# Gating one tile ahead and two output tiles inside the last RWKV tile, in a hybrid attention and RWKV-7 encoder layer

## The chip, the cores and the metric

The kernel runs on one core of a Trainium2 chip. The metric is the device time of one execution in microseconds (us). The engines are PE (TensorE, with PEld its weight loads), DVE (VectorE), ACT (ScalarE), POOL (GpSimd) and SP (SyncE, which here only issues DMAs). Each runs its own instructions in the order in which they were written, and they meet at semaphores.

## What is computed

One layer of a hybrid streaming encoder, for a prompt of 2048 rows and for eight running streams of 16 rows (128 sample rows). The input is normalised and projected once; half of the columns feed a chunked attention of 8 heads, the other half an RWKV-7 recurrence of 8 heads, and both results are gated and projected back.

```python
proj = rms_norm(h_p, norm_gain[l]) @ w_in[l]
att, rcols, g_r = split_projection(proj)
q, k, v, g_a = attn_qkv(att, q_norm_gain[l], k_norm_gain[l])
o_a = chunk_band_attention(q, k, v, rel_pos_bias[l])
o_r, S_p = rwkv_branch(rcols, prev, zeros, g_r, *rw)
h_p = h_p + merge_out(o_a, g_a, o_r, w_out[l], h_p.dtype)

def wkv_scan(...):          # the recurrence, one step per row and head
    sa = jnp.einsum('bhij,bhj->bhi', S, -kk_t)
    S = (S * w_t[:, :, None, :] + sa[..., None] * (kk_t * a_t)[:, :, None, :]
         + v_t[..., None] * k_t[:, :, None, :])
    y = jnp.einsum('bhij,bhj->bhi', S, r_t)

def merge_out(o_a, g_a, o_r, w_out, dtype):
    z = jnp.concatenate([o_a * jax.nn.silu(g_a), o_r], axis=-1)   # o_r holds its own silu gate
    return z @ w_out
```

The sample rows go the same way, each stream from its own cached keys, values and state.

## The kernel before, in words

All is float32. Large products are made as three: each operand is split into a high part (rounded by a copy on ACT) and a low part (what is left, by a subtraction on DVE or POOL), and hi·hi, hi·lo and lo·hi are added in PSUM. A block of 8 slices of 128 by 512 columns is so 24 products.

There are four phases in order, and between them each engine meets the others at a barrier while POOL clears the semaphores that the phase held (`clear_semaphores`, L64 to L74; the clear itself at L66 in the rows). If the numbers held are consecutive, one instruction clears the range; otherwise one instruction clears each.

1. `attention_phase` (to about 588 us): projection, attention over the prompt.
2. `rwkv_projection_phase` (589 to 901): the RWKV columns. On ACT its head loads the sigmoid table (L971), then splits weights and input.
3. `rwkv_phase` (904 to 1634, clears to 1640.4), described below.
4. `output_phase` (from 1640.5): for each of 17 tiles of 128 rows, the gated z is turned (PE L2311), split (ACT L2198, DVE L2236), multiplied by `w_out` (PE L2318, 48 products), added to the input (DVE L2245) and stored. ACT makes the silu (L2193), DVE the gating (L2232). Eight of the tiles also carry the attention of one sample stream each (L2330 to L2349).

`rwkv_phase` has 17 tiles: 16 of 128 prompt rows and the sample tile (`DEC` = 16, mode "s"). For each engine small generators write the instructions of parts of a tile: `mix` (decay, key gate, the sum for kk), `front` (scaled keys, Gram matrices), `back` (the recurrence itself), `tail` (group norm, bonus, y), `gates` (the silu gates' projection, 48 products in 12 blocks of 4, PE L2036). A generator yields a number, the place in the tile in us, ahead of each piece; `merged` (L1075) always takes the piece with the smallest number next. These numbers alone set the order of instructions on each engine; `tiles` (L1313) says which parts of which tiles run together: `back(t)`, `tail(t-1)`, `front(t+1)`, `mix(t+2)` and `gates(t+2)` (`AHEAD` = 2). Ahead of the first tile `first_gates` makes the gates of tiles 0 and 1, and the last four of the eight splits of the gate weights (ACT L1634, DVE L1802).

`back(t)` begins with the levels: five of them (three in the sample tile), each a product w (PE L1927), its mask (DVE L1737), a product q (PE L1936), a copy y_mat (ACT L1589) and a transpose of it (DVE L1741), so that one level goes round three engines. Then for both chunks of 64 rows come the right hand side, the solve (PE L1963), the state product (PE L2000), the state add on DVE and the read-out (PE L1970). In the sample tile each stream has its own state: DVE masks rows by stream (L1766), PE multiplies by all states (L1952), and at the end PE L2019 and DVE L1776, L1780 renew them.

Level 0 of the next tile needs at its front: z (DVE L1726, a masking with two SBUF inputs, behind POOL's `bm` L1477), y2 (DVE L1729, a transpose of z), and on PE, in order ahead of it, the turns of v (L1838, L1841), which need kk_n (DVE L1675) read first. The gate of the tile is copied by ACT (L1618), then the next x is rounded on ACT (L1613) and its low part made on POOL (L1521; on DVE L1808 in the prologue); the first gate block of the next tile waits for that part.

`tail(t)` is DVE L1786 to L1794, ACT L1602 to L1607, POOL L1501 to L1516, then four stores on SP. Tiles 15 and 16 have no gates; in their place `out` splits `w_out` (ACT L1647, DVE L1814), four slices in each, and in tile 16 it makes silu (ACT L1652) and the gating (DVE L1821) for output tiles 0 and 1, whose inputs SP loads (L1404 to L1406). `z_att` holds the o_att and o_rwkv rows.

## Time and profile before

| what | value |
|---|---|
| median of 3 runs (lowest, highest) | 1881.86 us (1880.72, 1885.09) |
| profiled execution, own time | 1879.3 us |
| its span | 1877.5 us |
| mean granted clock of PE | 0.968 |
| busy: PE, PEld, DVE, ACT, POOL | 93%, 76%, 46%, 42%, 18% |

The page divides the span into 40 equal slices of 46.9 us; each digit is a share in tenths (9 is 90% or more), PEclk the granted clock of PE:

```
PE   6999999999999997999999699999999999976389999
DVE  4345454445544412223445655566555665223432
ACT  4455655555555412223434444444434432014321
POOL 3010100100100000000214443345334532200000
PEclk9999999999999999999899999999999999986689999
```

Times of instructions are taken from one profiled execution and counted from the start of its span. A share of busy time is a mean over stages that have different limits, so each stage is read for itself. In a timeline, `[0.84 <-POOL gate_x_lo L1521]` says that the engine had been idle for 0.84 us and which event ended that.

### The profile page before, as it was taken

Reading aid. Unit: us, or ns where it says so; the run is one execution under the profiler, and the core shown is the slowest. Engines: PE = TensorE matmul, PEld = TensorE weight load, DVE = VectorE, ACT = ScalarE, POOL = GpSimd, SP = SyncE. Lnnn points to the kernel's source line nnn. Section 1 sums busy time; section 2 is a strip of 40 time slices with the busy share of each in tenths; the row PEclk is TensorE's granted clock in tenths of the full one; section 3 lists DMA queues with packets and bytes.
Section 4 is the critical chain, followed back from the end, with each engine's and each line's share of the span. In section 5 each row is a group of like instructions: output and inputs, shape, how many; then the busy total and the mean of one; then the engine's idle time right before and its main releaser. Section 6 shows DMA issues by size and latency. Waiting matters only on the chain. (4 is left out here: it accounts for less than half of the span.)

```text
span 1877.5 us, 48788 instructions
## 1 busy us (share of the span) xinstructions
PE 1740.1 (93%) x21474; PEld 1428.1 (76%) x21474; DVE 854.9 (46%) x1211; ACT 784.2 (42%) x1678; POOL 342.3 (18%) x249
## 2 busy tenths in 40 slices
PE   6999999999997999999699999999999976389999
PEld 4677778877886888999577777777777766267787
DVE  4345454445544412223445655566555665223432
ACT  4455655555555412223434444444434432014321
POOL 3010100100100000000214443345334532200000
PEclk9999999999999999999899999999999986689999
DMA  6010101101115322224212221121112123166642
GB/s 225 28 52 34 51 29 35 51 29 56 52 35 191 131 101 87 81 81 131 107 49 67 66 60 49 53 81 56 54 50 84 39 59 110 37 218 210 235 162 101
DMA packets 110977, 160.84 MB, mean 86 GB/s; under 512 B 36272, under 2 KB 73520, under 8 KB 110512
## 3 DMA queue, kind: packets, MB, share of 16 engines
q1 hardware_dynamic: 101408, 143.25, 23.3%
q10 hardware_dynamic: 9360, 14.49, 2.1%
q8 instruction: 170, 2.79, 0.6%
q14 instruction: 39, 0.32, 0.1%
HBM read 103.18 MB, written 55.05 MB: 84 GB/s over the span
## 5 line engine op out<-in xcount | busy, mean ns | idle before, releaser
L625 PE MATMUL a_ps_proj<-a_w_hi,a_x_hi 128*128 128x512 f32 x384 | 158.5, 413 | 2.9 <-ACT a_qk L374 2.8
L625 PE MATMUL a_ps_proj<-a_w_hi,a_x_lo 128*128 128x512 f32 x384 | 158.8, 414 | 0.0
L625 PE MATMUL a_ps_proj<-a_w_lo,a_x_hi 128*128 128x512 f32 x384 | 156.5, 408 | 0.0
L1045 DVE SCALAR_TENSOR_TENSOR j_out<-j_ps,j_rest,j_part 128x512 f32<-128x512 f32 (+2 forms) x65 | 41.9, 644 | 217.0 <-ACT j_last_cols L991 169.9
L2036 PE MATMUL r_ps_gate<-gate_w_hi,gate_x_hi 128*128 128x512 f32 x272 | 116.1, 427 | 21.4 <-POOL gate_x_lo L1521 11.8
L304 POOL TENSOR_TENSOR a_x_lo<-a_xT,a_x_hi 128x1024 fp32r<-128x1024 f32 x17 | 41.5, 2442 | 483.8 <-ACT a_x_hi L360 456.8
L2036 PE MATMUL r_ps_gate<-gate_w_hi,gate_x_lo 128*128 128x512 f32 x272 | 119.6, 440 | 0.0
L2036 PE MATMUL r_ps_gate<-gate_w_lo,gate_x_hi 128*128 128x512 f32 x272 | 115.8, 426 | 0.0
L2318 PE MATMUL o_ps_y<-out_w_hi,o_z_hi 128*128 128x512 f32 x272 | 111.5, 410 | 4.0 <-DVE o_y L2245 4.0
L524 DVE SCALAR_TENSOR_TENSOR a_stage<-a_ps_s,a_old_bias 128x1024 f32<-128x1024 f32 (+3 forms) x60 | 66.9, 1115 | 93.1 <-PE a_ps_s L652 93.1
L2318 PE MATMUL o_ps_y<-out_w_hi,o_z_lo 128*128 128x512 f32 x272 | 107.6, 395 | 0.0
L2318 PE MATMUL o_ps_y<-out_w_lo,o_z_hi 128*128 128x512 f32 x272 | 107.6, 395 | 0.0
L989 ACT ACTIVATE j_part<-j_last_cols,j_shift_in 128x1 f32<-128x1 f32 x65 | 19.2, 295 | 210.3 <-PE j_ps L1070 210.3
L1737 DVE TENSOR_TENSOR r_w_mat<-r_ps_w,consts 128x512 f32<-128x512 f32 x83 | 57.3, 691 | 106.8 <-PE r_ps_w L1927 106.8
L411 ACT ACTIVATE a_stage<-a_stage,a_small 128x640 f32<-128x640 f32 (+4 forms) x128 | 95.8, 752 | 2.1 <-DVE a_small L530 2.1
L421 ACT ACTIVATE a_stage<-a_ps_p 128x512 f32<-128x512 f32 (+3 forms) x120 | 60.1, 553 | 71.1 <-PE a_ps_p L671 71.0
L625 PEld LDWEIGHTS a_ps_proj<-a_w_hi,a_x_hi 128*128 128x128 f32 x384 | 72.9, 190 | 21.1 <-ACT a_qk L374 5.4
L652 PE MATMUL a_ps_s<-a_kT,a_qT 64*128 64x128 f32 (+3 forms) x592 | 83.0, 391 | 3.9 <-ACT a_kT L402 1.4
L1070 PE MATMUL j_ps<-j_x_hi,j_w_lo_ 128*128 128x384 f32 (+1 forms) x240 | 85.5, 356 | 0.0
L1070 PE MATMUL j_ps<-j_x_hi,j_w_hi_ 128*128 128x384 f32 (+1 forms) x240 | 85.5, 356 | 0.0
L1070 PE MATMUL j_ps<-j_x_lo,j_w_hi_ 128*128 128x384 f32 (+1 forms) x240 | 85.5, 356 | 0.0
L530 DVE TENSOR_REDUCE a_small<-a_stage 128x2 f32<-128x1280 f32 (+4 forms) x64 | 84.5, 1320 | 2.2
(302 smaller groups left out, 4406.5 us busy)
## 6 DMA issues: line engine op xcount, KB each, us to landing
xs<-scratch_xs_T SPq DMA_DIRECT2D x17, 832.0 KB, 6.2
scratch_xT<-a_xT SPq DMA_DIRECT2D x17, 512.0 KB, 4.7
raw<-scratch_xT SPq DMA_DIRECT2D x17, 512.0 KB, 7.6
scratch_gates<-r_gate_out SPq DMA_DIRECT2D x34, 256.0 KB, 2.4
z_gate<-scratch_gates SPq DMA_DIRECT2D x17, 512.0 KB, 4.5
a_x<-in_x_prompt SPq DMA_DIRECT2D x16, 512.0 KB, 4.5
o_x<-in_x_prompt SPq DMA_DIRECT2D x16, 512.0 KB, 4.8
out_y_prompt<-o_y SPq DMA_DIRECT2D x16, 512.0 KB, 2.9
```

The source lines that it names most:

```text
L304: nc.gpsimd.tensor_tensor(x_lo[n % 2][:], xT[:], x_hi[n % 2][:].bitcast(F32), ALU.subtract).then_inc(x_lo_ready, 1)
L411: nc.scalar.activation(probs[s % 2][:, e, lo * P:WIN], probs[s % 2][:, e, lo * P:WIN], ACT.Exp, bias=neg_max[s % 2][:, e:e + 1], accum_out ...
L421: nc.scalar.activation(pT[:, e, lo:SLOTS - 1, :], ps_p[:, e * 512 + lo * P:(e + 1) * 512].rearrange("p (j n) -> p j n", n=P), ACT.Copy).th ...
L524: nc.vector.scalar_tensor_tensor(out=out[:, :, lo * P:OLD], in0=ps_old[:, :, lo * P:OLD], scalar=SCALE, in1=old_bias[:, 2 * c:2 * c + 2, l ...
L530: nc.vector.tensor_reduce(neg_max[s % 2], out[:, :, lo * P:WIN], AX_X, ALU.max, negate=True).then_inc(max_ready, 1)
L625: mm = nc.tensor.matmul(ps_proj[:], a[n % 2][:, k, :], w[:, k, g * AW:(g + 1) * AW], start=(k == 0 and i == 0), stop=(k == KT - 1 and i == 2))
L652: return nc.tensor.matmul(out, qT[half, c, :], kT[half, c, r:r + b - a, :].rearrange("p j n -> p (j n)"), start=True, stop=True)
L1045: last = nc.vector.scalar_tensor_tensor(out=out[j][:, 0:n], in0=ps[j][:, 0:n], scalar=rest[:, c:c + 1], in1=part[j][:, 0:n], op0=ALU.mult, ...
L1070: mm = nc.tensor.matmul(ps[j][:, 0:n * P], w[c][:, k, :], x[g % 2][:, k, 0:n, :].rearrange("p a n -> p (a n)"), start=(k == 0 and m == 0), ...
L1737: nc.vector.tensor_tensor(w_mat, heads(ps_w[:]), level, ALU.mult).then_inc(w_ready, 1)
L2036: mm = nc.tensor.matmul(ps_gate[:], x[:, k, :], w[:, j, k, :], start=i == 0, stop=i == 3 * KT - 1)
L2318: mm = nc.tensor.matmul(ps_y[t % 2][:, cols], a[t % 3][:, k, :], w[:, k, cols], start=(k == 0 and i == 0), stop=(k == KT - 1 and i == 2))
```

## The change

- `clear_semaphores` clears each run of consecutive numbers with one instruction, however the numbers lie.
- Projection phase: the load of the sigmoid table moves from ahead of the first weight split to behind the second.
- `AHEAD` is 1. The prologue makes tile 0's gate only, and two of its four weight splits move ahead into the first stage of the prologue (22.5, 24), two to the second (10.2, 14.5). In each tile t from 0 to 15 the gates of t+1 are made. The last two gate blocks move from 30 and 31.5 to 28.9 and 30. kk_n (DVE) moves from 33.4 to 32.45, so that it stands ahead of y2.
- Tile 15 makes the gates of tile 16 where it split `w_out`. All eight splits of `w_out` stand in tile 16, with four buffers for the loads.
- In tile 16, `out` makes output tiles 0 and 1 whole: loads of gates and of both o, silu, gating, 16 transposes in groups of 4, splits, 96 products in blocks of 4 at the places of `OUT_AT` (two halves of 512 columns each, in the banks of the gate and of a job), the addition of x, and four stores. In the same tile z of output tiles 2 and 3 is prepared as that of 0 and 1 was. The second chunk's stream masks get the place 23, the two products for the new states 40 and 44.
- `output_phase` begins at tile 2, with the first sample stream on its second tile instead of its third.

```diff
             numbers = sorted(sem.num for sem in held)
-            if numbers[-1] - numbers[0] == len(numbers) - 1:
-                pool.sem_clear(range(numbers[0], numbers[-1] + 1))
-            else:
-                for sem in held:
-                    pool.sem_clear(sem)
+            first = numbers[0]
+            for now, after in zip(numbers, numbers[1:] + [None]):
+                if after != now + 1:
+                    pool.sem_clear(range(first, now + 1))
+                    first = after
...
-        self.out_w_loaded, self.out_w_hi, self.out_w_lo = [sem(f"out_w_loaded{i}") for i in range(2)], sem("out_w_hi"), sem("out_w_lo")
+        self.out_w_loaded, self.out_w_hi, self.out_w_lo = [sem(f"out_w_loaded{i}") for i in range(4)], sem("out_w_hi"), sem("out_w_lo")
...
-            act.preload_act_table_set("sigmoid_and_others")
             split_w(0)
             for k in range(KT):
                 split_x(0, k)
             split_w(1)
+            act.preload_act_table_set("sigmoid_and_others")
...
-        FIRST_GATES = ([(0, 0, 10)] + [(0, b, 16 + b) for b in (1, 2, 3)] + [(0, 4, 33)],
-                       [(0, 5, 10), (0, 6, 10.5), (0, 7, 12), (0, 8, 13)] + [(0, b, 10 + b) for b in (9, 10, 11)] +
-                       [(1, 0, 23), (1, 1, 23.5), (1, 2, 24)] + [(1, b, 23 + b) for b in (3, 4, 5)] + [(1, 6, 30), (1, 7, 30.5), (1, 8, 31)] +
-                       [(1, 9, 32), (1, 10, 33), (1, 11, 34)])
-        FIRST_GATES_OUT = ([], [(0, 0, 11), (0, 1, 22), (1, 0, 28.9), (1, 1, 34.5)])
-        GATE_W_AT = (13, 19, 22, 24)
-        OUT_AT = {DEC - 1: (5, 10, 15, 33), DEC: (1.5, 5.6, 9.7, 13.8)}
-
-        def out_blocks(t):
-            return range(4) if t == DEC - 1 else range(4, KT)
+        FIRST_GATES = ([(0, 10), (1, 17), (2, 18), (3, 19), (4, 33)],
+                       [(5, 10), (6, 10.5), (7, 12), (8, 13), (9, 19), (10, 20), (11, 21)])
+        GATE_W_AT = ((22.5, 24), (10.2, 14.5))
+        OUT_AT = (12, 13, 14, 15, 16, 17, 26.3, 26.4, 26.5, 33, 34, 35, 36, 37, 41, 42, 43, 43.5) + tuple(45 + i for i in range(6))
...
-        AHEAD = 2
+        AHEAD = 1
...
-                    run.append(out(t, u, "p"))
+                    run.append(out(t, u, "s"))
...
-            load_gate_x(2)
...
+            def load_out_w(k):
+                sp.dma_start(out_raw[k % 4][:].rearrange("p k n -> p (k n)"), io["w_out"][0, k * P:(k + 1) * P, :]).then_inc(shared.out_w_loaded[k % 4], 16)
+
+            def load_go(n, gate_loaded, att_loaded):
+                rows, b = slice(n * P, (n + 1) * P), n % 2
+                sp.dma_start(z_gate[b][:].rearrange("p g n -> p (g n)"), io["gates"][rows, :]).then_inc(gate_loaded, 16)
+                sp.dma_start(z_att[b][:, 0, :], io["o_att"][rows, :]).then_inc(att_loaded, 16)
+                sp.dma_start(z_att[b][:, 1, :], io["o_rwkv"][rows, :]).then_inc(att_loaded, 16)
...
+            def first_out():
+                for name in ("B1", "K1", "bonus", "kk_sum"):
+                    was_written(sp, DEC + 1, name)
+                for j in range(2):
+                    sp.wait_ge(gate_stored[j], 16 * 4)
+                sp.wait_ge(o_stored, 64 * 4)
+                load_go(0, go_loaded[0], go_loaded[0])
+                load_out_w(2)
+                load_out_w(3)
+                load_go(1, go_loaded[1], go_loaded[1])
...
+                yield 0
+                for k in range(4, KT):
+                    sp.wait_ge(shared.out_w_lo, k - 3)
+                    load_out_w(k)
+                for j in range(2):
+                    sp.wait_ge(gate_stored[j], 16 * (DEC + 1))
+                    load_x_half(0, j)
+                yield 19
+                for n in range(2):
+                    sp.wait_ge(z_turned, 2 * n + 2)
+                    load_go(2 + n, shared.g_loaded[n], shared.o_loaded[n])
+                for j in range(2):
+                    yield 31 + j
+                    store_y(0, j)
+                    sp.wait_ge(y_stored[j], 16)
+                    load_x_half(1, j)
...
+            def open_gates(n, loaded, opened):
+                act.wait_ge(loaded, 48 if loaded is go_loaded[n % 2] else 16)
+                nc.scalar.activation(z_gate[n % 2][:], z_gate[n % 2][:], ACT.Silu).then_inc(opened, 1)
...
+                yield 0.2
+                split_w(0)
+                split_w(1)
+                yield 1.4
+                open_gates(0, go_loaded[0], z_opened)
+                open_gates(1, go_loaded[1], z_opened)
+                yield 3.4
+                split_w(2)
+                split_w(3)
+                for n in range(2):
+                    for i in range(2):
+                        yield 6 + 2 * n + i
+                        round_z(n, i)
+                for k in range(4, KT):
+                    yield 10 + k
+                    split_w(k)
+                for n in range(2):
+                    yield 33 + n
+                    open_gates(2 + n, shared.g_loaded[n], shared.silu_ready)
...
-                yield 33.4
+                yield 32.45
...
+                            yield 23
...
+                yield 0.3
+                split_w(0)
+                split_w(1)
+                for n in range(2):
+                    yield 3 + n
+                    gate(n, z_gate[n], z_opened, z_gated)
+                yield 5.2
+                split_w(2)
+                split_w(3)
+                for n in range(2):
+                    for i in range(2):
+                        yield 6.4 + 2 * n + i
+                        split_z(n, i)
+                for k in range(4, KT):
+                    yield 10.5 + k
+                    split_w(k)
+                yield 27
+                add_x(0, 0)
+                yield 36
+                add_x(0, 1)
+                for n in range(2):
+                    yield 34 + n
+                    dve.wait_ge(shared.o_loaded[n], 32)
+                    gate(2 + n, z[n], shared.silu_ready, shared.z_ready)
...
+            for j in range(2):
+                add_x(1, j)
...
+                        yield (40, 44)[n]
...
-                for j, keys in enumerate(((1.1, 3.2, 5.2, 7.3, 9.3, 11.4), (13.4, 17.5, 19.6, 23.6, 30, 31.5))):
+                for j, keys in enumerate(((1.1, 3.2, 5.2, 7.3, 9.3, 11.4), (13.4, 17.5, 19.6, 23.6, 28.9, 30))):
...
+                def products(n, j, b):
+                    for i in range(4 * b, 4 * b + 4):
+                        k, m = divmod(i, 3)
+                        if i == 0:
+                            wait(pe, y_added, 2 * (n - 1) + j + 1)
+                            if n == 0:
+                                pe.wait_ge(z_lo_ready, 4)
+                                pe.wait_ge(gate_copied, 2 * (DEC + 1))
+                        if n == 0 and j == 0 and m == 0:
+                            pe.wait_ge(shared.out_w_lo, k + 1)
+                        a, w = ((z_hi, out_hi), (z_hi, out_lo), (z_lo, out_hi))[m]
+                        mm = nc.tensor.matmul(out_bank(j)[:], a[n][:, k, :], w[:, k, OUT_X[j]], start=i == 0, stop=i == 3 * KT - 1)
+                    if b == 5:
+                        mm.then_inc(y_summed, 1)
+
+                for n in range(2):
+                    for i in range(2):
+                        yield 6 + 2 * n + i
+                        turn(n, i)
+                for b, key in enumerate(OUT_AT):
+                    yield key
+                    products(b // 12, b // 6 % 2, b % 6)
...
-        FIRST = 2
+        TILE0, STREAM0 = 2, 1
+        LAST = DEC - TILE0
...
-            z_high(1)
-            silu(2)
-            z_high(2)
-            silu(3)
-
-            for t in range(FIRST, DEC + 1):
-                if t + 1 <= DEC:
+            for t in range(LAST + 1):
+                if t + 1 <= LAST:
...
-            turn(1)
             pe.wait_ge(w_lo_ready, KT)
-            for t in range(2):
-                pe.wait_ge(z_lo_ready, t + 1)
-                for j in range(2):
-                    for k in range(KT):
-                        products(t, j, k)
-            turn(2)
-
-            for t in range(FIRST, DEC + 1):
+            for t in range(LAST + 1):
```

In `out` on PE, `turn` waits for z_gated and the bank (`B1`, `K1` read, later z_lo of the group before), transposes four slices and signals z_turned. On ACT and DVE `round_z` and `split_z` make the high and low parts of each group of four slices, and `add_x(n, j)` adds the bank to the half of x that SP loaded. The PE part of `output_phase` no longer has its first two tiles ahead of the loop.

## Rows read from the trace of the kernel before

**Rows 1.** Windows: stretch, length, busy (x count) per engine, clock, DMA share, GB/s

```profile
1220.49:1258.42 37.93, 36.60 (x877) 29.40 (x868) 22.45 (x36) 17.08 (x36) 16.30 (x13) 1.00 0.21 60
1525.33:1563.07 37.74, 25.70 (x745) 23.95 (x737) 25.42 (x36) 13.11 (x24) 9.92 (x7) 0.76 0.24 72
1563.07:1602.29 39.22, 25.96 (x580) 24.40 (x582) 23.06 (x25) 9.88 (x15) 11.19 (x7) 0.62 0.33 105
1640.50:1675.96 35.46, 28.28 (x120) 23.42 (x121) 6.49 (x8) 6.35 (x6) 1.84 (x4) 0.84 0.48 174
904.00:953.86 49.86, 39.94 (x420) 29.80 (x424) 23.13 (x29) 21.97 (x42) 15.70 (x15) 0.87 0.25 91
```

**Rows 2.** Chain that ended last: start, length, engine, tile, line, count

```profile
1644.31 1.24 DVE o_z_lo L2236
...
1647.61 23.50 PE o_ps_y L2318 x96
...
1796.36 10.93 PE o_ps_y L2318 x48
```

**Rows 3.** SP queue's waits (total, times, longest), 1560 to 1700, then 580 to 600

```profile
SPq L66 <- PEq L66: 6.7, 1, 6.7
...
SPq L66 <- PEq L66: 0.5, 1, 0.5
```

**Rows 4.** Timeline, ACT, projection head: start, length, line, tiles, count, [idle, releaser]

```profile
589.00 1.28 ACT L971 ACT_TABLE_LOAD   x1 [4.63 <-PEq L66]
```

**Rows 5.** Timeline, DVE and POOL, prologue of the RWKV phase (904 to 955)

```profile
916.37 3.72 DVE L1802 TENSOR_TENSOR gate_w_lo<-raw,gate_w_hi 128x1024 fp32r<-128x1024 f32 x2 [0.70 <-ACT gate_w_hi L1634]
...
948.27 1.28 POOL L1463 TENSOR_TENSOR r_kmod<-xs,r_fac 128x512 f32<-128x512 f32 x1
...
948.35 1.75 DVE L1726 TENSOR_TENSOR r_z_mat<-r_bm,consts 128x512 f32<-128x512 f32 x1 [0.68 <-POOL r_bm L1477]
```

**Rows 6.** Waits of PE, 950 to 1525: waiter, releaser, total, times, longest

```profile
PE r_ps_gate L2036 <- POOL gate_x_lo L1521: 11.8, 14, 0.8
```

**Rows 7.** Timeline around one tile boundary (1215 to 1223): PE, DVE, POOL

```profile
1215.44 0.40 PE L2036 MATMUL r_ps_gate<-gate_w_lo,gate_x_hi 128*128 128x512 f32 x1
1215.77 0.68 PE L2000 MATMUL r_ps_s<-r_u_tok,r_b_tok 64*64 64x64 f32 x16
...
1218.05 0.39 PE L2036 MATMUL r_ps_gate<-gate_w_hi,gate_x_lo 128*128 128x512 f32 x1
...
1222.50 0.50 PE L2036 MATMUL r_ps_gate<-gate_w_hi,gate_x_hi 128*128 128x512 f32 x1 [0.84 <-POOL gate_x_lo L1521]
...
1217.29 0.69 DVE L1726 TENSOR_TENSOR r_late<-r_late,consts 128x512 f32<-128x512 f32 x1
...
1218.65 0.65 DVE L1675 TENSOR_SCALAR r_kk_n<-r_ps_job 128x512 f32<-128x512 f32 x1
...
1220.09 2.35 POOL L1521 TENSOR_TENSOR gate_x_lo<-raw,gate_x_hi 128x1024 fp32r<-128x1024 f32 x1 [3.89 <-ACT gate_x_hi L1613]
```

**Rows 8.** Timeline of tile 16 (1563 to 1634): ACT, DVE, POOL

```profile
1567.87 0.60 ACT L1589 ACTIVATE r_y_mat<-r_ps_q 128x512 f32<-128x512 f32 x1 [6.21 <-PE r_ps_q L1936]
...
1591.72 1.28 ACT L1652 ACT_TABLE_LOAD   x1
1593.01 2.00 ACT L1652 ACTIVATE z_gate<-z_gate 128x1024 f32<-128x1024 f32 x2
...
1579.37 5.03 DVE L1766 TENSOR_TENSOR r_late<-r_ar,consts 128x512 f32<-128x512 f32 x4
...
1594.99 1.21 DVE L1814 TENSOR_TENSOR out_w_lo<-raw,out_w_hi 128x1024 fp32r<-128x1024 f32 x1
...
1616.18 0.69 DVE L1776 TENSOR_TENSOR r_states<-r_states,r_ps_s 128x512 f32<-128x512 f32 x1 [7.23 <-PE r_ps_q L2019]
...
1627.93 1.26 POOL L1516 TENSOR_TENSOR r_y_tok<-r_y_tok,r_y_sq 128x512 f32<-128x512 f32 x1
```

**Rows 9.** DMA issues of 1565 to 1620: count, KB each, median us to landing

```profile
z_att<-scratch_o_rwkv SPq DMA_DIRECT2D x2, 256.0 KB, 7.0
```

More of the change, by code:

```diff
@@ L1437, in _ @@
             tiles(sp, nothing, back, mix, tail, gates, first_gates, out)
+            for j in range(2):
+                store_y(1, j)
+            for j in range(2):
+                sp.wait_ge(y_stored[j], 16 * 2)
             sp.wait_ge(stored, 16 * (1 + NCH))
@@ L1810, in out, with add_x, split_w @@
+                if t == 1:
+                    yield 24.6
+                    dve.wait_ge(x_hi_ready, 2)
+                    nc.vector.tensor_tensor(x_lo[:], x_raw[1][:], x_hi[:].bitcast(F32), ALU.subtract).then_inc(x_lo_ready, 1)
+            def add_x(n, j):
+                dve.wait_ge(y_summed, 2 * n + j + 1)
+                dve.wait_ge(x_half_loaded[j], 16 * (n + 1))
+                nc.vector.tensor_tensor(gate_out[j][:], gate_out[j][:], out_bank(j)[:], ALU.add).then_inc(y_added, 1)
             def out(t, u, mode):
-                for k in out_blocks(t):
-                    yield OUT_AT[t][k % 4] + 1.1
+                def split_w(k):
@@ L2047, in first_gates, with out, turn @@
             def first_gates(t, u, mode):
-                for n, b, key in FIRST_GATES[t]:
+                for b, key in FIRST_GATES[t]:
                     yield key
-                    gate_products(n, b // 6, b % 6)
-            tiles(pe, front, back, mix, gates=gates, first_gates=first_gates)
+                    gate_products(0, b // 6, b % 6)
+            def out(t, u, mode):
+                def turn(n, i):
+                    pe.wait_ge(z_gated, n + 1)
+                    if n == 0:
+                        was_read(pe, DEC, ("B1", "K1")[i])
+                    else:
+                        pe.wait_ge(z_lo_ready, 2 * n - 1 + i)
+                    for k in range(4):
+                        last = nc.tensor.transpose(ps_job[i][:, k * P:(k + 1) * P],
+                                                   z_gate[n][:].rearrange("p g d -> p (g d)")[:, (4 * i + k) * P:(4 * i + k + 1) * P], ident)
+                    last.then_inc(z_turned, 1)
+                def products(n, j, b):
[3 more added lines that the diff above has]
+                            wait(pe, y_added, 2 * (n - 1) + j + 1)
+                            if n == 0:
+                                pe.wait_ge(z_lo_ready, 4)
[13 more added lines that the diff above has]
+                    products(b // 12, b // 6 % 2, b % 6)
+            tiles(pe, front, back, mix, gates=gates, first_gates=first_gates, out=out)
 def output_phase(nc, io, shared):
@@ L2280, in _ @@
             split_z(0)
-            split_z(1)
-            apply(2)
-            split_z(2)
-            place_queries()
-            add(0, 0)
-            add(0, 1)
-            add(1, 0)
-            for t in range(FIRST, DEC + 1):
-                add(t - 1, 1)
-                if t + 1 <= DEC:
+            for t in range(LAST + 1):
+                if t > 0:
+                    add(t - 1, 1)
+                if 2 <= t + 1 <= LAST:
                     apply(t + 1)
@@ L2299, in _ @@
                     bias_and_max(b)
-                if t + 1 <= DEC:
+                if t + 1 <= LAST:
                     split_z(t + 1)
+                if t == 0:
+                    place_queries()
                 add(t, 0)
-            add(DEC, 1)
+            add(LAST, 1)
         @block.tensor
```

160 lines of the change are left out of this document (78 added, 82 removed).

## The prediction

> **What bounds the kernel now.** The profiled execution took 1879.3 us for a span of 1877.5 us; the median of the runs is 1881.86 us, 2.6 above it. All sums are differences on that execution, and I apply the total to the median.
>
> I read the 40 slices first (they stand in the section on the profile: PE at nine tenths nearly everywhere, with a hole from 1500 to 1690), then the stretches of the RWKV phase in a table by windows [rows 1], then the timeline around each hole, engine by engine. A steady RWKV tile lasts 37.93 us and PE is busy for 36.60 of them: it is bound by PE. The last two tiles are not. Tile 15 has PE busy for 25.70 of 37.74 at a granted clock of 0.76, tile 16 (the sample tile) for 25.96 of 39.22 at 0.62; here the level chain, going round PE, DVE and ACT, sets the time. Then come the last states, the tail and the store, 6.7 us with nothing on any engine, and 35.46 us until the output phase starts its third tile. The output phase itself is a chain on PE alone: 48 products in 10.93 us, 0.227 each [rows 2].
>
> **Output phase.** It loses tiles 0 and 1 from its head: 96 products in 23.50 us, their turns, and the wait for add, turn and split of tile 2. Before, tile 2's first product starts 35.46 us after the phase does [rows 1]. Now tile 2 is what tile 0 was: its low part is written 1644.31 + 1.24 = 5.1 us after the phase's start at 1640.5 [rows 2]. Gain 35.46 - 5.1 = 30.4. The clock's climb costs about the same in both (96 products took 23.50 where 96 x 0.227 = 21.8). Eight stream tiles and seven plain ones follow in either kernel. The loads lie closer to their first use; landing within 8 us of issue (the slowest like row is 7.0 [rows 9]) they keep ahead of tile 3, 15 us in. Bounds 27 to 32.
>
> **Semaphore clears.** Before the output phase, the queue of SP waited 6.7 us; at the same point after the attention phase, whose numbers are consecutive, 0.5 [rows 3]. By runs, the RWKV phase should cost like the latter: gain 6.2. If the numbers lie scattered, nothing; I know no reason for more than a few runs.
>
> **Projection's head.** ACT loads its table for 1.28 us before the first weight split, with PE idle behind it [rows 4]. Moved behind the second split, it delays only the third split, which PE wants ten us later. Gain 1.3.
>
> **Prologue.** Two things. The four weight splits no longer stand ahead of the first tile's chain on DVE (two of them took 3.72 us [rows 5]): the scan starts 3 us earlier, but the first two now sit in front of kk_n and the other two lengthen ACT's and DVE's queues in the next stage, so 2.6 us remain at the turns of b. Then the whole of tile 1's gate (48 products, 10.9 us by [rows 2]) is gone from between the turns and level 0, 13.5 together. The work behind it shows through: ACT's copies of k, of the gate and of b and the split of x, five times 512 columns at 0.6 [rows 8], and on DVE the masking of z, 1.75 behind POOL as now [rows 5], and kk_n. Laid end to end these are 5.4; walked through the Gram steps and the turns, 5.0 of them lie bare. Level 0 starts at 945.3 where it now starts at 953.86 [rows 1]. Gain 8.5; bounds 7 and 11.
>
> **Steady tiles.** Now PE waits at each tile's head for POOL's low part of x: 11.8 us in 14 tiles [rows 6]. The last two gate blocks move ahead of the solve and ahead of the state product, so the gate is copied and x split sooner and this wait goes. But the state product comes later, and with it the state add, z, kk_n and the turns that must precede level 0. Let L be the start of the last gate product. The state product follows at L + 0.33 (as 1215.44 to 1215.77), z at 1.52 behind it (1215.77 to 1217.29), L + 1.85; kk_n, now ahead of y2, at z's end, 0.64 later; level 0, behind the turns, 1.84 after kk_n (1218.65 to 1220.49): L + 4.33 [rows 1, 7]. Counting the blocks that move ahead of it, I put L at 1216.7 where the row has 1218.05, so level 0 starts at 1221.05 (now 1220.49), and the next gate block at 1222.2 (now 1222.50). Gain 0.3 per tile, 14 times, and 0.7 at the boundary before tile 15, which now has z lengthened by POOL: 4.9. Bounds 0 and 10.
>
> **Tile 15** gains a gate (11 us of PE) in 12 us of idle PE, a full clock, and loses four w_out splits that made PE wait. The levels become those of a steady tile. Less the mix of a tile 17 that does not exist and plus DVE's slower sample forms I estimate 36.7 against 37.74: gain 1, bounds -1 and 3.
>
> **Tile 16** takes it all up: 96 products (21.8 us), 16 transposes, all eight w_out splits, four z rounds, four splits, four gate products, two silu pairs, four adds and all their DMAs. T is the start of its level 0, before at 1563.07 [rows 1]. The places where it ends up on the path:
> - ACT waits in order for the gates of both tiles. SP can issue them only behind the last gate's store; with w_out's blocks between, tile 1's last load is issued at T + 1.2 and lands after 7.0 [rows 9]: T + 8.2. The silu follows, and only then the first y_mat copy, at T + 9.3 instead of 4.8 [rows 8]: +4.5.
> - The other two levels, with transposes, z rounds, w_out splits, and the tail of tile 15, which now loads two tables: +2.6.
> - DVE's stream masks (5.03 us) are followed in order by w_out blocks 4 to 7 at 1.21 each [rows 8], and PE by the products that need them. The first stream product starts at T + 34; before, it followed the masks' end, T + 21.3. Together with the above: +12.6.
> - Back by the clock: stream products, solve and read-out of both chunks take 1.5 to 2 us less each, while 12 products stand between them: +9.9 at the end of the read-out.
> - 20 products ahead of the first key product and 16 ahead of the second: their PE time hides the wait for POOL, mostly. The second states' add starts at T + 65 instead of 53.1 [rows 8]: +11.8.
> - The tail is unchanged (POOL ends it at 1629.2 [rows 8]); two y stores are queued on SP behind it: +1.1.
> - The idle head again runs at half clock in part: +1.1.
> Cost 14, bounds 6 and 22.
>
> A table load is followed at once by its silu (1.28 us, next start 0.01 later [rows 8]). The Trainium skill, "ScalarE: Activation LUTs", section "What ACT_TABLE_LOAD costs", gives about 2.66 us for a switch with its drain; by that the three loads that tile 16 gains would cost ACT 4.1 us more than by the row (an estimate from that page), and the time would be up to 4 us later. The row speaks against it.
>
> **Sum.** -30.4 - 6.2 - 1.3 - 8.5 - 4.9 - 1 + 14 = -38.3: a span of 1839 and a median of 1881.9 - 38.3 = 1843.6.
>
> **Rivals.**
> A. The sample tile costs more: the loads land as late as 10 us, or DVE's w_out splits stand between masks and state work a second time; PE then waits for products with its clock down. Price 10 to 12 on top: about 1855. For it: every filler there sits in order ahead of the chain. Against: the 13.3 us in which PE was idle in that tile before [rows 1].
> B. DVE loses the race at each tile's end. When POOL's instruction runs, DVE's z (two SBUF inputs) is finished only after POOL's: started 0.08 later, it took 1.75 us instead of 0.69, ending 0.55 behind POOL [rows 5, 7]. After the change POOL's split of x (2.35 us) is ready to start at L + 2.04 and z at L + 1.85: DVE leads by 0.2. If POOL is first, z ends 2.4 us later and each tile costs 2.1 instead of gaining 0.3: 15 x 2.4 = 36 us, 1880. If PE's idle 3 us there also pull the clock down, as in tile 15 with its idle stretches (0.76 against 1.00 [rows 1]), the small products that follow slow down too, 1 to 2 us per tile more: 1895 to 1910, slower than before. It decides at one point, 0.2 us less lead. The trace's tiles repeat to 0.05 us, so I hold it unlikely. The Trainium skill's "GPSIMD Engine Reference", section "Key points", says that GpSimd shares its SBUF interfaces with VectorE and contends with instructions of two SBUF inputs; the trace agrees, and by that rule alone either order is open.
> C. The sample tile costs only 6 and the steady tiles gain 0.8 (kk_n early enough that PE hardly waits): 1827.
> D. The clears are not shortened, since the numbers do not form few runs: 1850.
>
> **Chances.** The forecast with its small errors (1836 to 1852) 0.53; D inside it or by itself 0.05; A 0.20; C 0.12; B 0.10, of which 0.04 near 1880 and 0.06 above. From 1830 to 1862 lie 8 in 10. About 0.2% is what a measurement of this kernel tells from no change; faster by more 0.90, within 0.04, slower 0.06.
>
> **What the profile will show.** The output phase's first product 5 us after its start; SP's wait at the clear near 0.5; level 0 of tile 0 near 944; tile period 37.6 with z at 0.69 and x's low part behind it; a full clock in tile 15; in tile 16 ACT's first y_mat copy behind the silu, and the stream products 34 us in. A z above 1.5 us in the steady tiles would be B. Wrong by more than 15 us would be the tile 16 walk or B.

## The result and the profile after

The changed kernel has a median of 1870.01 us (1863.60 to 1879.61, 18 runs), the kernel before 1881.19 us over as many runs (1876.43 to 1885.09). The ratio is 0.9945, 95% interval 0.9929 to 0.9961: 11 us faster, where 38 had been forecast, and outside the stated range. The profiled execution took 1877.1 us for a span of 1875.3 us; it is one of the slower ones, 7 us above the median. The sums below are made on its span against the 1877.5 of before.

The stretches of the changed kernel, by windows (columns as in [rows 1]): all tiles from level 0 of tile 0 to that of tile 15, tile 15, tile 16 to the end of the clears, the output phase, then two bad tiles and a good one. These last three are cut at one and the same point, 0.8 us behind the tile's gate store on SP.

```profile
946.38:1540.91 594.53, 566.36 (x13001) 448.50 (x12995) 324.14 (x537) 254.85 (x522) 238.41 (x172) 0.98 0.19 55
1540.91:1577.43 36.52, 33.62 (x792) 26.88 (x785) 22.04 (x33) 12.31 (x24) 12.91 (x11) 1.00 0.19 58
...
1577.43:1669.22 91.79, 56.95 (x752) 44.93 (x752) 43.07 (x48) 23.70 (x32) 21.70 (x14) 0.79 0.35 121
1669.22:1875.30 206.08, 199.14 (x1184) 158.84 (x1184) 70.48 (x116) 60.16 (x69) 1.84 (x4) 0.98 0.54 192
1172.09:1214.91 42.82, 38.65 (x867) 30.68 (x866) 21.83 (x37) 17.10 (x36) 16.57 (x12) 0.96 0.18 53
1408.31:1453.43 45.12, 39.98 (x867) 31.39 (x866) 21.83 (x37) 17.06 (x36) 16.57 (x12) 0.92 0.17 50
1134.51:1172.09 37.58, 36.89 (x867) 29.27 (x866) 21.80 (x37) 17.07 (x36) 16.59 (x12) 1.00 0.20 61
```

The first thing to read is the last three lines. They do the same work (867 products each), and take 37.58, 42.82 and 45.12 us. The good tile is what was forecast. Of the 15 tile periods, taken from one first mask of level 0 to the next, six are 37.6 to 37.7, three 38.1 to 38.8 and six 40.2 to 43.4. (The stop of the tile of 45.12 lies ahead of its mask, so by the masks it is shared out between that tile and the one before.) By terms:

| term (us, + is slower) | forecast | measured on the two traces |
|---|---|---|
| output phase | -30.4 | 206.1 against 237.0: -30.9 |
| semaphore clears | -6.2 | SP's wait 0.9 against 6.7: -5.8 |
| projection's head and prologue | -9.8 | level 0 at 946.38 against 953.86: -7.5 |
| steady tiles | -4.9 | 594.53 against 571.47: +23.1 |
| tile 15 | -1 | 36.52 against 37.74: -1.2 |
| tile 16 to the output phase, less the clears | +14 | 90.9 against 70.7: +20.2 |
| sum | -38.3 | -2.1 (spans: -2.2) |

The sum is 36 us off, and two lines carry 34 of them: 28 in the steady tiles and 6 in tile 16. Now the waits of PE from 960 to 1540 in the changed kernel; these two are the largest. "Issue" is time in which the engine waited for nothing that the profile shows.

```profile
PE r_ps_q L2031 <- issue: 11.3, 4, 3.5
PE r_ps_w L2022 <- issue: 6.4, 4, 4.4
```

The wait for POOL's low part of x [rows 6] is gone, as forecast; 17.7 us of "issue" stand where before there was 0.7. The timeline of the head of one bad tile, PE, ACT and SP's queue:

```profile
1171.29 0.33 SPq L1375 DMA_DIRECT2D scratch_gates<-r_gate_out  x1
1171.73 0.38 SPq L1354 DMA_DIRECT2D xs<-scratch_xs_T  x1
1172.15 0.86 SPq L1360 DMA_DIRECT2D raw<-scratch_xT  x1
...
1176.78 0.33 PE L2031 MATMUL r_ps_q<-r_w_mat,r_z_mat 64*64 64x64 f32 x3
...
1180.58 1.86 PE L2031 MATMUL r_ps_q<-r_w_mat,r_z_mat 64*64 64x64 f32 x29 [3.47 <-issue]
...
1182.48 0.60 ACT L1628 ACTIVATE r_y_mat<-r_ps_q 128x512 f32<-128x512 f32 x1 [7.57 <-PE r_ps_q L2031]
```

PE issues 3 of the 32 products of one group and then none for 3.5 us. Inside such a group there is no semaphore: nothing that the kernel wrote makes it wait there. What it can lack is instructions. The page's DMA section has a queue for them, and the DMA view shows it in a window from 1166 to 1178 (first fence) and in the microsecond after it (second fence).

```profile
DMA  0000000000000000000059978669899689999984
...
q1 hardware_dynamic: 1957, 1.62, 44.9%
```

```profile
q8 instruction: 1, 0.02, 6.6%
q1 hardware_dynamic: 11, 0.02, 5.4%
```

Over the kernel it moves this (packets, MB, share):

```profile
q8 instruction: 170, 2.79, 0.6%
```

2.79 MB in 170 packets are 16.4 KB each; PE has 21474 products and as many weight loads, 65 bytes for each instruction. So q8 carries PE's instructions in pages of some 256. The Trainium skill's page "Runtime: NRT & Kernel Launch", section "Instruction fetch mechanics", says that each engine takes its instructions from a FIFO which its sequencer refills in blocks of 16 KiB, 256 instructions, over a DMA queue of its own; the packets agree. It also says that the cost of a block border is mostly hidden, and that PE's store holds 2048 instructions, while two lines on it speaks of two blocks only. Here the border is not hidden. And PE had run dry 5.8 us after the burst's start, of which it had issued 132 products in the first 5, some 270 instructions; a store of 2048 would have lasted for a whole tile (1734 products and loads). The measurement decides, and it fits two blocks (below).

From 1166 to 1178 no page starts; the 1.6 MB that SP issues at the tile's head (256 KB of gates, 832 KB of xs, 512 KB of x) keep the DMA engines busy for 6 us. The next page starts at 1178.11, when the burst is over, and PE goes on at 1180.58. Here are the starts of the pages' packets around some heads of tiles, in us from the gate store's issue. The last column is the time from the next page's start to PE's going on.

| tile's gate store at | page before | next page | gap | PE's stop | PE goes on after |
|---|---|---|---|---|---|
| changed, 1332.28 | -1.9 | +6.7 | 8.6 | none | |
| changed, 1294.59 | -3.1 | +5.9 | 9.0 | none | |
| changed, 981.51 | -3.7 | +6.6 | 10.3 | 1.0 | 2.4 |
| changed, 1214.11 | -4.9 | +6.6 | 11.5 | 2.6 | 2.3 |
| changed, 1171.29 | -5.6 | +6.8 | 12.4 | 3.5 | 2.5 |
| before, 1332.87 | -5.4 | +2.0 | 7.4 | none | |
| before, 1219.09 | -3.6 | +5.1 | 8.7 | none | |
| before, 1142.24 | -4.2 | +6.1 | 10.4 | 0.7 | 2.4 |

In the main, the longer the gap, the longer the stop; it is no strict rule, since a gap of 12.1 went with the longest stop (4.4), and one of 9.8 in the kernel before with none. Two things mark the stops. The traces of both kernels and of the later runs have 37 stops of 0.4 us or more at the heads of tiles. In all of them PE goes on 2.2 to 2.7 us after the start of the next page. And in 36 of them PE had issued 440 to 500 products and loads since the start of the page before (in the last one, of 0.5 us, 372): close to two pages, since PE's waits for semaphores take places in a page too (128 of them move the stops to other tiles, below). So PE stops when the pages that it holds are used up, and goes on when the next has come.

In five of the tiles 1 to 14 of before a page still starts in the first 4 us of the burst, in the changed kernel in one. The page borders drift against the tiles by some 0.8 us a tile, so the bad tiles come in series. After a stop of 2.2 us or more the granted clock falls (0.96 and 0.92 for those tiles; 1.00 otherwise, after the stops of 1.0 us too), which adds to the price: the tile of 3.5 us of stop is 5.2 longer than a good one.

### The profile page after: what moved, and what is told of

The parts are those of the page before. It is cut to its first block and busy times, and to the rows that moved or that the text cites. A ratio compares the mean times of both kernels' runs of the same rounds, so it can differ in the third digit from the quotient of the medians.

```text
span 1875.3 us, 48713 instructions
## 1 busy us (share of the span) xinstructions
PE 1752.0 (93%) x21474; PEld 1425.8 (76%) x21474; DVE 846.3 (45%) x1212; ACT 788.4 (42%) x1683; POOL 348.5 (19%) x250
## 3 DMA queue, kind: packets, MB, share of 16 engines
q1 hardware_dynamic: 101984, 143.25, 23.1%
q8 instruction: 170, 2.79, 0.6%
## 5 line engine op out<-in xcount | busy, mean ns | idle before, releaser
L2441 PE MATMUL o_ps_y<-out_w_hi,o_z_hi 128*128 128x512 f32 x240 | 98.2, 409 | 2.5 <-DVE o_z_lo L2364 2.5
L2441 PE MATMUL o_ps_y<-out_w_hi,o_z_lo 128*128 128x512 f32 x240 | 94.4, 393 | 0.0
L2441 PE MATMUL o_ps_y<-out_w_lo,o_z_hi 128*128 128x512 f32 x240 | 94.4, 393 | 0.0
```

Source lines behind the costliest of these rows:

```text
L2441: mm = nc.tensor.matmul(ps_y[t % 2][:, cols], a[t % 3][:, k, :], w[:, k, cols], start=(k == 0 and i == 0), stop=(k == KT - 1 and i == 2))
```

## The experiments

Twelve kernels ran. Runs of before stood beside each group; their medians were 1882.0, 1879.7 and 1880.5.

**Moving a number that moves nothing.** The first two tries were meant to take x out of the burst:

```diff
             def gates(t, u, mode):
-                yield 0.5
+                yield 0.5 if t == DEC else 12
                 sp.wait_ge(x_lo_ready, t + (t == DEC))
```

> Theory (page): PE takes its instructions in pages of 16 KB by DMA, and in the changed kernel a page that falls due at a tile's head waits for the burst of 1.6 MB (gate store, xs, x) that begins there; PE stands still 1 to 4.5 us in 7 of 15 tiles. Here the 512 KB load of x moves from the place 0.5 to 12, so the burst is a third shorter. Expected: no stall above 1 us, tile period 37.6, about 25 us less than the changed kernel's profiled 1877 (near 1850), and less scatter. Rival (clock or another cause inside PE): stalls as before, 1865 to 1880.

> The same move of the x load in the kernel before. Page theory: it had one stall of 1.0 us in its trace, so 0 to 2 us less, 1880. If a shorter burst helped for another reason (bandwidth of the loads themselves), it should gain here as much as in the changed kernel.

Measured: 1865.9 (1859.6 to 1875.8) and 1882.0 (1878.8 to 1884.0); the trace of the first has nearly the same stops as the changed kernel's (12.0 us at q, 2.7 at w): in tiles 6, 7 and 8 they are 3.1, 2.6 and 0.8 us against 3.5, 2.6 and 0.7. SP has nothing between the places 0.5 and 12 in its own order, so the order of its instructions, and of every engine's, is that of the changed kernel and of the kernel before. These two runs are repeats; they decide nothing on the theory, but the first shows that the stops stay in their tiles from one execution to another. A place in this kernel orders a queue; only something waited for delays it.

**Shifting the page borders.** 128 waits that are already fulfilled, ahead of PE's first instruction of the phase:

```diff
             pe.wait_ge(params_loaded, 32)
-            pe.wait_ge(set_up, 5)
+            for _ in range(128):
+                pe.wait_ge(set_up, 5)
```

> The changed kernel with 128 waits that are already fulfilled added ahead of PE's first instruction of the RWKV phase: half a page of instructions, nothing else. Page theory: the page borders shift by half a page against the tiles, so other tiles stall (about 3 tiles off those of before), as many in number; total within 10 us of the changed kernel. Rival (stall belongs to certain tiles or to data): the same tiles stall.

Measured: 1883.2 (1872.4 to 1892.1), ratio 1.001 (0.9992 to 1.0028), 13 us slower than the changed kernel. PE's "issue" time in the same stretch of its trace:

```profile
PE r_ps_q L2032 <- issue: 11.2, 4, 3.5
PE r_ps_w L2023 <- issue: 6.3, 3, 4.9
```

The stops are as many and as long, and most sit in other tiles: the masks of level 0 lie more than 40 us apart after tiles 1, 2, 8, 9, 13 and 14, where the changed kernel's trace has tiles 6, 7, 11, 12, 13 and 14. The series of 3.5, 2.6 and 0.7 us in tiles 6, 7 and 8 stands, as 3.5, 2.4 and 0.9, in tiles 8, 9 and 10: two tiles on, where about three had been expected. So a stop belongs to a place in the instruction stream and not to a tile or its data. The pad is not free, which I had not reckoned with: PE's wait at the start of the phase is 12.9 us instead of 6.0, and those 6.9 us are half of the 13; the other half is not in that trace.

**The keys put back.** The change moved the last two gate blocks; this undoes only that and the place of kk_n.

```diff
-(13.4, 17.5, 19.6, 23.6, 28.9, 30)
+(13.4, 17.5, 19.6, 23.6, 30, 31.5)
...
-                yield 32.45
+                yield 33.4
```

> The changed kernel with the last two gate blocks back at 30 and 31.5 and kk_n back at 33.4. Page theory: state product to level 0 takes 4.7 us again instead of 3.0, a page of small products lasts longer, so the burst is over before the next one is due: stalls vanish or stay under 1 us, period 37.95 as before; sum: 15 x 0.35 us dearer, 25 us of stalls less: near 1855. Rival (stalls come from the gates one tile ahead or the new prologue): stalls stay, 1870 to 1885.

Measured: 1857.7 (1853.6 to 1859.5), ratio 0.9874 (0.9857 to 0.9891), 12 us faster than the changed kernel. Its trace has no line of "issue" for PE from 960 to 1540; the wait of before is back instead:

```profile
PE r_ps_gate L2132 <- POOL gate_x_lo L1560: 12.5, 15, 0.9
```

All its periods are 37.8 to 38.2. The gates one tile ahead and the new prologue are not the cause.

**The reverse, in the kernel before.**

```diff
-(13.4, 17.5, 19.6, 23.6, 30, 31.5)
+(13.4, 17.5, 19.6, 23.6, 28.9, 30)
...
-                yield 33.4
+                yield 32.45
```

> The kernel before with nothing but the changed kernel's keys for the last two gate blocks (28.9, 30) and for kk_n (32.45). Page theory: PE's stretch from state product to level 0 is compressed, so stalls of 1 to 4 us appear at some tiles' heads while the others take 37.6: 1880 to 1895, slower than before. Rival (the stalls need the gates one tile ahead): 5 us faster than before, 1877.

Measured: 1896.8 (1893.5 to 1909.3), ratio 1.0103 (1.0067 to 1.0139). Three numbers make the kernel before 17 us slower. Its PE, 960 to 1540:

```profile
PE r_ps_q L1936 <- issue: 10.7, 4, 3.2
PE r_ps_w L1927 <- issue: 1.3, 2, 0.8
```

What these three numbers do to the burst is seen in the timelines. SP's gate store waits for the copy of the last gate product, and xs and x are queued behind it. With the block at 31.5 (before, and keys put back) the store is issued 2.6 us ahead of DVE's mask of level 0, with the block at 30 (changed, and this run) 4.5 us ahead. Between the store and level 0, PE has the turns of v in the one case (1.4 us), in the other also the sum for kk and the read-out (3.3 us). PE is not denser in the burst (some 132 products in the first 5 us of it in either kernel): the burst has moved against the stream, by 1.9 us, so that another page falls due in it. Ahead of it now stand the gate blocks, over which, as I read it, a page lasts longer: the page before a bad burst starts up to 5.8 us ahead of it, in the kernel before up to 4.3 where the next one came at the burst's end. Why some pages of before get through in the burst's first 4 us is not settled by these traces.

**The burst taken away, keys left.** First x alone goes behind the first gate store of the tile, which waits for a copy some 13 us in; then xs also waits for the tile's first q product.

```diff
                 for j in range(2):
                     yield (13.2, 33.5)[j]
                     store_gates(t, j)
+                    if t < DEC and j == 0:
+                        sp.wait_ge(x_lo_ready, t)
+                        load_gate_x(t + 1)
...
                 yield 0.1
+                sp.wait_ge(q_written, LP * (t - 2) + 1)
                 was_written(sp, t - 1, "v_tok")
```

> Changed kernel, with the 512 KB load of x placed behind the first gate store of its tile on SP, which waits for a gate copy 13 us into the tile, so that it really leaves the burst at the tile's head (a mere change of its number left SP's order, and so the burst, as it was). 1.1 MB remain in the burst. Page theory: stalls shrink from up to 4.4 us to 0 to 2, median 1855 to 1865. Rival (stall has nothing to do with the loads): stalls as in the changed kernel, 1866 to 1875.

> As the run before it, and the 832 KB load of xs waits for the first q product of the tile, so that only the 256 KB gate store is left at the tile's head. Page theory: no stall above 0.8 us at the head, all tiles 37.6 to 37.7, and with the changed kernel's own keys 5 us less than with the keys put back (1857.7): near 1852. Rival: no better than the changed kernel, or new stalls where the burst now lies.

Measured: 1856.6 (1851.5 to 1862.2), ratio 0.9886 (0.9857 to 0.9915), with x late; 1851.4 (1849.0 to 1853.8), ratio 0.9849 (0.9834 to 0.9865), with both. PE's "issue" in the first is this, and the second has no such line in the stretch:

```profile
PE r_ps_q L2032 <- issue: 3.4, 3, 1.7
```

SP's queue at the head of a tile in the second, now 6.7 us from the gate store to xs:

```profile
1214.14 0.33 SPq L1375 DMA_DIRECT2D scratch_gates<-r_gate_out  x1
1220.82 0.38 SPq L1354 DMA_DIRECT2D xs<-scratch_xs_T  x1
1231.39 0.32 SPq L1375 DMA_DIRECT2D scratch_gates<-r_gate_out  x1
1231.77 0.42 SPq L1360 DMA_DIRECT2D raw<-scratch_xT  x1
```

All its periods are 37.57 to 37.82, and the tiles' whole stretch (mask to mask, tile 0 to 15) takes 564.5 us against 570.8 of before: a gain of 6.4 where 4.9 was forecast. The page follows the burst's end as the burst gets shorter. In tiles 1 to 14 the first page that starts later than 0.8 us behind the gate store does so at 5.9 to 7.2 us with 1.6 MB at the head, at 4.5 to 6.0 with x late (1.1 MB) and at 3.2 to 5.1 with both late (0.25 MB). With the burst and the early keys there are stops, with either one gone there are none or hardly any. That is what makes the two together the cause.

> The same with 128 fulfilled waits ahead of PE's first instruction, half a page. Page theory: with the burst away from the dense stretch the place of the page borders does not matter: within 5 us of the run without the pad, where the pad cost 13 us in the changed kernel. Rival (the pad itself costs 13 us, or stalls are bound to page borders alone): 10 us or more slower than without.

Measured: 1859.6 (1853.1 to 1860.6), 8 us slower than without the pad, of which 6.9 are the waits themselves by the trace above; its own trace shows no stop at a tile's head over 0.2 us. The time lies between what the two sides had named (within 5 us, or 10 and more); the trace decides. With the burst away the place of the borders no longer makes PE stop at the tiles' heads, while in the changed kernel it decides which tiles stop. Its other three runs lie 6 to 8 us above the profiled one, and what they spent is not in a trace: this stays open.

**The clears alone**, on the kernel of the two late loads.

> The stall-free kernel (loads of xs and x late, 1851.4) with the old way of clearing semaphores. The clears' term was put at 6.2 and the changed kernel's trace shows SP waiting 0.9 us there instead of 6.7: 5 to 6.5 us slower than 1851.4, 1857. Rival (the numbers form one run, or clears hide beside the last stores): within 1 us.

Measured: 1858.3 (1852.5 to 1861.3), 6.9 more. Two medians of four runs that scatter by 5 and 9 us would be weak alone; the wait itself is in the traces. SP's wait at the clear, with the old way (first fence) and by runs (second):

```profile
SPq L66 <- PEq L66: 7.6, 1, 7.6
```

```profile
SPq L66 <- PEq L66: 0.9, 1, 0.9
```

From POOL's last y to the output phase it is 13.7 us against 6.9. The term was right.

**Tile 16.** The chain at its head in the changed kernel, ACT, and at its middle DVE and PE:

```profile
1581.55 1.06 ACT L1683 ACTIVATE z_gate<-z_gate 128x1024 f32<-128x1024 f32 x1 [3.49 <-DMA z_att<-scratch_o_rwkv]
1588.26 1.06 ACT L1683 ACTIVATE z_gate<-z_gate 128x1024 f32<-128x1024 f32 x1 [5.65 <-DMA z_att<-scratch_o_rwkv]
1589.22 0.58 ACT L1628 ACTIVATE r_y_mat<-r_ps_q 128x512 f32<-128x512 f32 x1
...
1604.06 7.01 DVE L1829 TENSOR_TENSOR r_late<-r_ar,consts 128x512 f32<-128x512 f32 x4
1611.00 2.35 DVE L1879 TENSOR_TENSOR out_w_lo<-raw,out_w_hi 128x1024 fp32r<-128x1024 f32 x2
1613.27 2.35 DVE L1879 TENSOR_TENSOR out_w_lo<-r_out_raw,out_w_hi 128x1024 fp32r<-128x1024 f32 x2
...
1617.56 2.08 PE L2047 MATMUL r_ps_rhs<-r_states,r_late 64*64 64x64 f32 x64
```

Level 0 starts at 1577.43. The first y_mat copy is behind the second silu, as forecast, but at T + 11.8 and not T + 9.3 (the last load is issued at T + 2.6 instead of 1.2 and takes 8.2 us instead of 7.0); the first stream product starts at T + 40.1 and not T + 34; the second new states' add at T + 71.9 and not T + 65. Two edits, alone and together: SP loads both output tiles' gates and o before two slices of w_out instead of around them, and the 12 products that wait for w_out's last low parts move behind the first stream products.

```diff
                 load_go(0, go_loaded[0], go_loaded[0])
+                load_go(1, go_loaded[1], go_loaded[1])
                 load_out_w(2)
                 load_out_w(3)
-                load_go(1, go_loaded[1], go_loaded[1])
...
-        OUT_AT = (12, 13, 14, 15, 16, 17, 26.3,
+        OUT_AT = (12, 13, 14, 23, 24, 25, 26.3,
```

> The stall-free kernel with SP's loads at the end of tile 15 in another order: the gates and o of both output tiles first, two slices of w_out behind them instead of between. Theory (ACT's first y_mat copy of tile 16 is queued behind the second silu, whose loads land last of 4 MB at 11 us into the tile): copy at 8 instead of 11.8, 2 to 4 us faster, 1848. Rival (the first w products wait for w_out slices, or the delay is made up by DVE's masks): no change.

> The stall-free kernel with that move of 12 products alone, loads in the changed kernel's order: 4 to 6 us faster than 1851.4, 1846, if the two gains are independent.

> As the run before it, and the 12 output products of the places 15 to 17 move to 23 to 25, behind the first chunk's stream products and solve. Theory (they wait for w_out's last low parts, which DVE makes 4.7 us behind the masks, and hold the stream products up): stream products start at the masks' end, 5 to 6 us sooner; another 4 to 6 us faster, 1843. Rival (DVE's second masks then wait behind the same splits, or the solve is delayed instead): under 2 us.

Measured: loads alone 1848.6 (1845.8 to 1852.0), ratio 0.9831 (0.9815 to 0.9847); products alone 1849.9 (1845.8 to 1857.3), ratio 0.9842 (0.9810 to 0.9873); both 1845.1 (1844.6 to 1846.8), ratio 0.9813 (0.9798 to 0.9829). In the traces, from the first mask of tile 16 to the output phase's start: 89.2 with neither, 84.6, 84.7 and 82.8. Without either edit this stretch takes 87.7 to 89.8 in eight traces (among them the one with the old clears, less 6.7), so each edit alone brings 3 to 5 and the two together 5 to 7: they share part of the gain. By the medians each edit alone brings 2.8 and 1.5, within the scatter of four runs; the second had been given 4 to 6, and the two together 4 to 6 beyond the first, where 3.5 came. The trace with both:

```profile
1558.62 1.06 ACT L1685 ACTIVATE z_gate<-z_gate 128x1024 f32<-128x1024 f32 x1 [1.85 <-DMA z_att<-scratch_o_rwkv]
1559.58 0.58 ACT L1630 ACTIVATE r_y_mat<-r_ps_q 128x512 f32<-128x512 f32 x1
...
1574.44 7.02 DVE L1831 TENSOR_TENSOR r_late<-r_ar,consts 128x512 f32<-128x512 f32 x4
...
1585.01 0.38 ACT L1634 ACTIVATE r_rhs<-r_ps_rhs 128x256 f32<-128x256 f32 x1 [8.02 <-PE r_ps_rhs L2049]
```

The copy stands 5.4 us behind the first mask (at 1554.17) instead of 9.8, the right hand side 30.8 instead of 40.3. One thing in the trace of the loads alone speaks for caution: two steady tiles took 39.1 and 39.3 and PE has this line again, though only the gate store is left at the tile's head. In both the next page starts 3.2 us behind the store, 8.8 us after the one before it.

```profile
PE r_ps_w L2024 <- issue: 2.7, 2, 1.4
```

So the late loads make the stops rare and small, and do not exclude them.

The kernel with all four edits, 1845.1 us, is 1.9% faster than the kernel before and 25 us faster than the changed one.

## Why the prediction was wrong, step by step

**What bounds the kernel** was right for the steady tile as the traces of good tiles show it, and incomplete: I took PE's instructions for granted. The trace of before had the sign: one boundary lasted 38.93 instead of 37.93, with PE idle on "issue" for 0.7 us, and I had passed over it.

**Output phase**: -30.9 against -30.4 (the phase took 234.8 to 237.0 us in the three traces with the old one, 205.7 to 206.4 in the eleven with the new). The low part of its first z is done 5.0 us after its start, the first product starts 5.1 us after it. Right.

**Clears**: -5.8, and 6.9 in the run that undid them alone. Right.

**Projection's head and prologue**: -7.5 against -9.8. The projection's head gives 0.6 net by the end of that phase; the attention phase had ended 0.4 later in this execution. In the prologue 7.0 came, at my lower bound of 7, for a forecast of 8.5: more of the chain behind the removed gate lay bare than my walk had it. The walk took the times of the rows, while the granted clock from the last instruction of the projection phase to the first mask fell from 0.87 to 0.72; how much of the missing 1.5 us this is has not been separated. The gain is not a fixed one either. That stretch takes 54.6 us in all three traces with the old prologue, and with the new one 47.8 to 49.8 in seven traces of unpadded kernels, but 51.1 and 51.2 in two. z took 1.74 behind POOL, as forecast.

**Steady tiles**: this step failed. Its arithmetic was sound: a good tile gains 0.35 where I said 0.3, x's low part starts behind z as I wanted it,

```profile
1214.91 0.68 DVE L1788 TENSOR_TENSOR r_late<-r_late,consts 128x512 f32<-128x512 f32 x1
...
1215.11 2.72 POOL L1560 TENSOR_TENSOR gate_x_lo<-raw,gate_x_hi 128x1024 fp32r<-128x1024 f32 x1 [2.59 <-ACT gate_x_hi L1652]
```

and with the burst out of the way the stretch gained 6.4. The lead of DVE over POOL is the 0.2 us that I had worked out, in all 15 tiles, so rival B did not come true in any. What I left out is what the moved blocks release. The gate copy frees SP's queue: its store, xs and x followed it 1.9 us sooner against level 0. I counted the PE, DVE, ACT and POOL work behind the moved blocks and not the three DMAs, although they are queued behind the very copy that I moved. Their collision with PE's pages cost 29 us in the profiled execution, and by the medians of keys put back and of both loads late 12 to 19 us.

**Tile 15**: -1.2 against -1. Full clock, as forecast. Right.

**Tile 16**: the mechanisms were the ones I named and all were under-priced: 20.2 against 14, inside the bounds of 6 and 22. The loads of the gates and o landed as late as 8.2 us after issue, with 4 MB under way together (rival A had 10); the masks took 7.01 and not 5.03, with POOL running the tail of tile 15 beside them (7.01 or 7.02 in all eleven traces of the changed kernel and its variants); and the twelve products that I had queued behind w_out's low parts hold the streams until T + 40.1. With two orders changed the stage, from its first mask, takes 82.8 less 0.9 for the clears, against 75.4 less 6.7 before: a cost of 13.2.

**Rival A** was thus right in part (6 of its 10 to 12). **Rival C** is in no run: without the burst a tile gains the forecast 0.35 and not 0.8, and tile 16 cost 13 at best and not 6. **Rival D** is refuted.

**The forecast** of 1843.6 was wrong for what the change gave as written. The kernel with both loads late, which is this change without the burst, gave 1851.4, 8 us above the forecast: tile 16 makes 6 of them and the prologue 2. That 1845.1 was reached in the end, near the forecast, took two more edits in tile 16 which the forecast did not have, and is in that respect luck. None of my cases had a stop of PE for lack of instructions; the range ended at 1862 and the measured median lay 8 us above it.

**Open**: the spread of the changed kernel (16 us over 18 runs, before 9) fits a page that races a burst, but only two executions of it are in traces, this one and the repeat. The scatter of 6 to 12 us left in four of the kernels with both loads late is explained in part: the attention phase, which no kernel here changes, ends between 585.9 and 589.7 us in the 14 traces, and the new prologue's stretch takes 47.8 to 51.2. Why these two vary is open. How large a burst PE bears was only bounded: with 1.1 MB there are stops up to 1.7 us, with 0.25 MB up to 1.4 in one trace and none over 0.2 in five.

## What to carry to other kernels

When a step moves, ask which DMAs its result releases and what the other engines do in the microseconds in which these run; an unrolled kernel of small products needs a page of instructions every 5 us or so (about seven in a tile of 37.6 here) and gets it through the same DMA engines. A wait on "issue" in the middle of a group of like products was a missing page here: look for the burst beside it, and delay the loads by something that is waited for, since a later place in the queue alone delays nothing. Work that fills idle time is queued in order ahead of the chain: 12 products put a few places too early here held up the whole tile for their own operands.

## What was unexpected of the hardware

- PE stood still for up to 4.4 us (4.9 in the padded kernel) within a group of products, with no semaphore to wait for; its next instruction page had started only at the end of a burst of 1.6 MB, up to 12.4 us after the one before it (12.5 in the padded kernel).
- PE had then issued 440 to 500 products and loads since the page before, in 36 of 37 stops, and went on 2.2 to 2.7 us after the next page's start.
- 128 waits that were already fulfilled cost PE 6.9 us, 54 ns each (12.9 against 6.0).
- Four stream masks on DVE took 5.03 us in the kernel before and 7.01 beside four POOL instructions with SBUF inputs (two in the kernel before).
- A stop of 3.5 us cost the tile 5.2, with the granted clock at 0.96 for the tile.
